# Mixer projections placed between attention units, ada slabs shared out anew, and expert slabs loaded in pairs, in a two-block transformer kernel

## The reference

```python
for l in range(DEPTH):
    mod = (silu(c) @ ada_w[l] + ada_b[l]).reshape(B, 3, 3, D)      # 9 x 1024 columns
    x = x + 0.5 * mod[:, 0, 2] * swiglu(modulate(rms_norm(x), ...), ffn_w_in[l, 0], ffn_w_out[l, 0])
    x = x + mod[:, 1, 2] * token_mix(modulate(rms_norm(x), ...))
    x = x + 0.5 * mod[:, 2, 2] * swiglu(modulate(rms_norm(x), ...), ffn_w_in[l, 1], ffn_w_out[l, 1])
```

```python
y_gdn = gated_deltanet(qkv, z, b_raw, a_raw, ...)   # causal convolution of 4 taps, silu, l2 norms,
                                                    # chunked delta rule over 4 heads of 128, norm, * silu(z)
y_nsa = native_sparse_attention(q, kc, vc, ks, vs, kw, vw, gates, ...)   # 8 heads of 64, rotated
                                                    # three branches: compressed (15 keys), selected, window
return concatenate([y_gdn, y_nsa]) @ w_out
```

## Time and profile before

| | |
|---|---|
| median of 3 runs | 3339.81 us (3338.42 to 3344.32) |
| profiled execution, its own time | 3344.84 us |
| its span | 3343.1 us |
| PE busy | 2922.2 us (87%) |
| DVE busy | 1452.7 us (43%) |
| ACT busy | 787.7 us (24%) |
| slab transfers | 662 of 1024 KB, 2 of 128 KB; 13.4 us from issue to landing |
| read from HBM | 697.84 MB |

### The profile page before, as it was taken

How to read it: one execution, slowest core, us unless ns; L and a number is a source line. 1 busy time by engine, 2 the same in 40 slices (tenths; PEclk the granted TensorE clock), 3 DMA queues, 4 the chain that set the end, 5 groups by cost and what they waited for, 6 DMA issues and landing times.

```text
span 3343.1 us, 43275 instructions
## 1 busy us (share of the span) xinstructions
PE 2922.2 (87%) x17606; PEld 2132.8 (64%) x17606; DVE 1452.7 (43%) x3244; ACT 787.7 (24%) x1477; POOL 0.2 (0%) x4
## 2 busy tenths in 40 slices
PE   6999776699999977679999998998988987999998
PEld 5998675599899867559987565333334675433333
DVE  3867433377676742336521313333333343233333
ACT  3331222243333122224322221101101232110100
POOL 0000000000000000000000000000000000000000
PEclk9999785699999978569999558999999997999999
DMA  8766300156466520014442002999997221799997
GB/s 318 277 232 233 117 1 26 36 210 235 188 254 251 227 101 12 15 41 153 185 148 92 1 9 114 384 420 421 421 421 300 76 102 51 315 421 421 421 421 327
DMA packets 99372, 701.77 MB, mean 210 GB/s; under 512 B 11744, under 2 KB 14176, under 8 KB 14304
## 3 DMA queue, kind: packets, MB, share of 16 engines
q1 hardware_dynamic: 99168, 698.93, 52.5%
HBM read 697.84 MB, written 1.05 MB: 209 GB/s over the span
## 4 chain that ended last, share of the span: by engine, by line
PE 42%; DMA 12%; DVE 4%; ACT 2%; issue 1%; SPq 0%; DVEq 0%; ACTq 0%
DMA ring<-slabs 12%; PE ps L1071 8%; PE ps L684 7%; PE ps L1092 4%; PE ps L1109 3%; PE ps L865 2%; PE ps L678 2%; PE ps L1282 2%; PE ps L1283 2%; PE ps L1284 2%; PE ps L1041 1%; PE ps L852 1%; PE ps L835 1%; PE ps L839 1%; PE ps L1239 1%
## 5 line engine op out<-in xcount | busy, mean ns | idle before, releaser
L1282 PE MATMUL ps<-arena_parts 128*128 128x256 f32 x2112 | 603.1, 286 | 24.1 <-DVE arena_parts L2739 24.1
L1283 PE MATMUL ps<-arena_parts 128*128 128x256 f32 x2112 | 599.1, 284 | 0.0
L1284 PE MATMUL ps<-arena_parts,ring_parts 128*128 128x256 f32 x2112 | 598.2, 283 | 0.0
L1071 PE MATMUL ps<-ring,arena 128*64 128x512 f32 x2048 | 471.6, 603 | 52.7 <-DMA ring<-slabs 47.8
L684 PE MATMUL ps<-h,ring 128*128 128x256 f32 (+1 forms) x1920 | 457.9, 400 | 19.2 <-DVE h L2383 7.6
L684 PEld LDWEIGHTS ps<-h,ring 128*128 128x128 f32 x1920 | 377.2, 198 | 88.1 <-issue 10.9
L1282 PEld LDWEIGHTS ps<-arena_parts 128*128 128x128 f32 x2112 | 403.6, 191 | 25.5 <-issue 25.3
L1284 PEld LDWEIGHTS ps<-arena_parts,ring_parts 128*128 128x128 f32 x2112 | 402.7, 191 | 0.0
L1283 PEld LDWEIGHTS ps<-arena_parts 128*128 128x128 f32 x2112 | 401.9, 190 | 0.2
L1071 PEld LDWEIGHTS ps<-ring,arena 128*64 128x64 f32 x2048 | 148.2, 138 | 302.3 <-issue 296.6
L2655 DVE TENSOR_TENSOR ring_parts<-ring,arena_parts 128x2048 fp32r<-128x2048 f32 x132 | 299.7, 2290 | 91.0 <-ACT arena_parts L1425 91.0
(11 more groups left out here) (347 smaller groups left out, 2773.7 us busy)
## 6 DMA issues: line engine op xcount, KB each, us to landing
ring<-slabs SPq DMA_DIRECT2D x662, 1024.0 KB, 13.4
constants<-const SPq DMA_DIRECT2D x1, 1372.5 KB, 7.6
x<-xT SPq DMA_DIRECT2D x1, 1024.0 KB, 9.8
outT<-x SPq DMA_DIRECT2D x1, 1024.0 KB, 4.7
vectors<-vec SPq DMA_DIRECT2D x1, 747.5 KB, 4.6
ring<-slabs SPq DMA_DIRECT2D x2, 128.0 KB, 5.5
arena<-pos SPq DMA_DIRECT2D x1, 128.0 KB, 7.4
x<-metaT SPq DMA_DIRECT2D x1, 64.0 KB, 9.8
```

What stands on the lines that cost most here:

```text
L1071: mm = nc.tensor.matmul(ps[W * hh:W * hh + W, e % 2, :], xe[:, e % 2, 4 * k + c], wt[:, c], start=(k == 0 and c == 0), stop=(k == 1 and c ...
L1282: nc.tensor.matmul(out, w_hi, v_hi, start=start, stop=False, skip_group_check=True)
L1283: nc.tensor.matmul(out, w_hi, v_lo, start=False, stop=False, skip_group_check=True)
L1284: return nc.tensor.matmul(out, w_lo, v_hi, start=False, stop=stop, skip_group_check=True)
```

## The change

**Mixer.** The order of the slabs becomes `MIX_ORDER`: first the six slabs of the attention (`nq`, `nk`, `vc`, `vtok`, `gba`: 14 jobs), then four of `qkv`, the two of compression, two of `qkv`, two of `z`. After the 14 jobs comes the rotation, then jobs and attention units alternate on PE: jobs 14 and 15; six times one job and one piece; two compression jobs with a piece each; eight times one job and two pieces. A piece is `scores(n + 1)`, `turn(n)`, `values(n - 1)`. Branches go 1, 2, 0. Then `gdn`. DVE puts one convolution ahead of each `softmax_max`, ACT the eviction of the job ahead of `exp`. The attention of the mixer uses banks 4 and 5 for scores, 6 for turns and 7 for values, one set each, because jobs hold 0 to 3. Its output lies in `hid`, its norm and turn are done inside `gdn` after levels 0, 1 and 2. Silu of `z` and of the compression's hidden values no longer happens in the eviction: `z` follows in `gdn` (ACT), the hidden values by an exponential on ACT and three steps on DVE (`hidden_cmp`).

**Ada slabs.** 16 instead of 12 in each of three FFNs, at two a step for the first six steps; 8 in mixer 0, 4 in mixer 1.

**Expert slabs.** Two neighbouring `eup` or `edown` slabs are one transfer of 2 MB, 16 KB a partition, which waits until both slots are free and counts on the even slot's semaphore. There are 192 of them, and 280 single slab loads.

The diff, cut to its core (the forgetting attention keeps its banks and its order):

```diff
+FFN_SHARE = 16
+MIX_ADA = ((1, 1, 2, 2, 1, 1), (1, 1, 1, 1, 0, 0))
+MIX_ORDER = (8, 9, 10, 11, 12, 13, 0, 1, 2, 3, 4, 5, 6, 7)
 def ada_share(l, i, step):
-    for at, layer, first in (((0, 0), 0, ADA_PART), ((0, 1), 1, 0), ((1, 0), 1, ADA_PART)):
+    for at, layer, first in (((0, 0), 0, ADA_PART), ((0, 1), 1, 0), ((1, 0), 1, FFN_SHARE)):
         if (l, i) == at:
-            past = lambda n: first + min(2 * n, n + 2, ADA_PART)
+            past = lambda n: first + min(2 * n, n + FFN_SHARE - 10, FFN_SHARE)
...
         elif st[0] == "mix":
-            for s in range(14):
-                out += [("mixin", st[1], s, "pe")]
-                out += [("ada", st[1], 2 * ADA_PART + s, "dve")] if s < ADA_PART else []
-            out += [("cmpw", st[1], s, "pe") for s in range(2)]
+            for p, i in enumerate(MIX_ORDER):
+                out += [("cmpw", st[1], s, "pe") for s in range(2)] if p == 10 else []
+                out += [("mixin", st[1], i, "pe")] + [("ada", st[1], n, "dve") for n in mix_share(st[1], p)]
...
+def paired(plan, i):
+    return plan[i][0] in ("eup", "edown") and plan[i + 1:i + 2] and plan[i + 1][0] in ("eup", "edown") and i % 2 == 0
...
             def load(i):
                 if i >= RING:
                     name, value = free[i - RING]
                     sp.wait_ge(s[name], value)
+                if paired(plan, i):
+                    name, value = free[i + 1 - RING]
+                    sp.wait_ge(s[name], value)
+                    both = ap["slabs"][i:i + 2].rearrange("n p w -> (n p w)").rearrange("(p w) -> p w", p=P)
+                    sp.dma_start(ring[:, i % RING:i % RING + 2, :].rearrange("p n w -> p (n w)"), both)\
+                        .then_inc(slot_loaded[i % RING], 16)
+                    return
...
# PE, mixer
-                    run_jobs(q, st, 0, 30, slab, job, h_at=("h_ready", n_ready - KC))
...
+                    run_jobs(q, st, 0, 14, slab, job, h_at=("h_ready", n_ready - KC))
+                    n_mix = sum(MIX_ADA[st[1]])
+                    mix_cols(q, st, sum(MIX_ADA[st[1]][:4]), n_mix)
...
                     pe.wait_ge(s["ada_col"], n_share)
+                    pe.wait_ge(s["proj_act"], act_before(q) + 8)
                     nsa_rope(q, st[1])
-                    await_("dve", q, "roped", 3)
+                    scores, piece, n_units = attention(q, st)
+                    for i in range(8):
+                        run_jobs(q, st, 14 + i, 15 + i, slab, job)
+                        if i == 1:
+                            await_("dve", q, "roped", 3)
+                            scores(0)
+                        elif i >= 2:
+                            piece(i - 2)
+                    await_("act", q, "kc2")
+                    for c in range(2):
+                        run_jobs(q, st, 22 + c, 23 + c, slab, job)
+                        piece(6 + c)
+                    nsa_compressed(q, st[1], job)
+                    for i in range(8):
+                        if i == 2:
+                            await_("act", q, "cmp")
+                        run_jobs(q, st, 24 + i, 25 + i, slab, job)
+                        piece(8 + 2 * i)
+                        piece(9 + 2 * i)
+                    piece(n_units)
+                    await_("dve", q, "o", n_units - 1)
                     gdn(q, st[1])
                     await_("dve", q, "y_gdn")
-                    await_("act", q, "kc2")
-                    run_jobs(q, st, 30, 32, slab, job)
-                    nsa_compressed(q, st[1])
-                    await_("act", q, "cmp")
-                    attention(q, st)
-                    turn_outputs(q, st)
                     await_("act", q, "y_att", 1)
                     run_jobs(q, st, 32, 40, slab, job, behind=True)
...
# ACT, mixer
+                    for i in range(8):
+                        evict(24 + i)
+                        for n_unit in (8 + 2 * i, 9 + 2 * i):
+                            exp(n_unit)
+                            copy(n_unit)
+                    gdn(q, st[1])
...
# ACT, gdn
+                act.wait_ge(s["proj_act"], act_before(q) + 26)
+                mark(nc.scalar.activation(view(ZS, 4, T1), view(ZS, 4, T1), ACT.Silu), q, "z")
                 nc.scalar.preload_act_table_set("natural_log_exp_and_others")
...
+                    if lev == 1:
+                        nsa_root(q)
+                    if lev == 2:
+                        take_outputs(q, ("mix", l))
...
# DVE, mixer
+                        softmax_max(0)
+                        for i in range(2, 8):
+                            conv(q, l, i)
+                            softmax_max(i - 1)
+                            if i > 2:
+                                output(i - 3)
...
+                        hidden_cmp(q, 0)
+                        hidden_cmp(q, 1)
+                        for i in range(8):
+                            if i < 4:
+                                conv(q, l, 8 + i)
+                            for n_unit in (8 + 2 * i, 9 + 2 * i):
+                                if n_unit < 23:
+                                    softmax_max(n_unit + 1)
+                                output(n_unit - 1)
+                        output(23)
+                        gdn(q, l, job)
...
# DVE, gdn, after each level
+                    if lev < 2:
+                        nsa_square(q, lev)
+                    if 1 <= lev < 3:
+                        nsa_scale(q, lev - 1)
```

More of the change, by code:

```diff
@@ L349, in host_arrays @@
         v = slab_array(s, a)
-        slabs[i, :, :v.shape[1]] = v
+        if paired(plan, i) or (i and paired(plan, i - 1)):
+            slabs[i - i % 2:i - i % 2 + 2].reshape(P, 2, SLAB)[:, i % 2] = v
+        else:
+            slabs[i, :, :v.shape[1]] = v
     return {
@@ L378, in build @@
     plan = slab_plan(stages)
-    free = releases(plan)
+    free, arrive = releases(plan), arrivals(plan)
     with ExitStack() as ctx:
@@ L467, in _ @@
             for i in range(len(plan)):
-                load(i)
+                if not (i and paired(plan, i - 1)):
+                    load(i)
             name, value = x_written(stages)[-1]
@@ L868, in values, with piece @@
                     mark(mm, q, "pv", n)
-                scores(0)
-                for n in range(len(units) + 1):
+                def piece(n):
                     if n + 1 < len(units):
@@ L877, in attention @@
                         values(n - 1)
+                return scores, piece, len(units)
             def turn_outputs(q, st):
@@ L1387, in _ @@
                     await_("act", q, "ncum")
-                    attention(q, st)
+                    scores, piece, n_units = attention(q, st)
+                    scores(0)
+                    for n_unit in range(n_units + 1):
+                        piece(n_unit)
                     turn_outputs(q, st)
@@ L1898, in _ @@
-                    gdn(q, st[1])
-                    nsa_blocks(q, st[1], job)
-                    hc, cb = view(HC, 2, 2 * NCMP), view(CB, 2)
+                        dst = {"qkv": lambda: qi[:, idx, 3:], "nq": lambda: nqk[:, idx], "z": lambda: zs[:, idx],
+                               "nk": lambda: nqk[:, 4 + idx], "vc": lambda: view(VC, T1)}[kind]()
+                        nc.scalar.copy(dst, bank((job + i) % 4, T1)).then_inc(s["proj_act"], 1)
+                    for i in range(14):
+                        evict(i)
@@ new lines, in _ @@
+                    nc.scalar.preload_act_table_set("natural_log_exp_and_others")
+                    gba_read = job_read[proj_end(q) - 1]
+                    act.wait_ge(s[gba_read[0]], gba_read[1])
+                    mark(nc.scalar.activation(view(SMALL + 128, 2, 28), view(SMALL, 2, 32)[:, :, 0:28], ACT.Exp,
+                                              scale=-1.0), q, "sg")
+                    exp, copy = attention(q, st)
+                    evict(14)
+                    evict(15)
+                    nsa_blocks(q, st[1], job)
@@ L1913, in _ @@
-                    attention(q, st)
-                    nsa_root(q)
-                    take_outputs(q, st)
+                    mark(nc.scalar.copy(view(VCMP, 2 * 64)[0:NCMP], ps[0:NCMP, (job + 23) % 4, 0:2 * 64]), q, "cmp")
+                    for i in range(8):
[4 more added lines that the diff above has]
+                    gdn(q, st[1])
                     for i in split_seq(q + 1, stages[q + 1])[0:2]:
@@ L1920, in _ @@
                     fox_forget(q)
-                    attention(q, st)
+                    exp, copy = attention(q, st)
+                    for n_unit in range(len(attn_units(st))):
+                        exp(n_unit)
+                        copy(n_unit)
                     take_outputs(q, st)
@@ new lines, in _ @@
+                        ada_col(l, 3 * ADA_PART - sum(MIX_ADA[l]), 3 * ADA_PART, ada_slabs)
+                        n_ada += 1
+                        nsa_rope(q, l)
+                        sg = view(SMALL + 128, 2, 28)
```

(5 more changed lines are left out.)

310 lines of the change are left out of this document (170 added, 140 removed).

## The result

The changed kernel takes **3239.1 us** (median of 4 runs, 3236.9 to 3241.0), the kernel before 3342.1 beside it (4 runs): ratio **0.9688**, 95% interval 0.9668 to 0.9709. It is faster, and inside the range of the forecast, but 103 us were saved where 157 were forecast.

The account below looks back on a forecast made before the run. PE bounds the dense stages, DMA holds the last expert stages, and no engine is full in the mixers' attention. Savings 72 + 78 + 5.4 - 4.8 + 6.3 = 157 us give 3183 us against the median; range 3145 to 3250.

Parts of the forecast that it names:

- term 6: Mixer, delta rule: silus, squares and table loads before the first root take 8.5 us; from there to its end 107.3.
- rival A: Clock stays at 1.2 GHz through the mixed stage: 90 us more per mixer, 3363 us in all; chance 4%.
- term 4: Mixer, two compression jobs: 7 us each at full clock, plus units, hidden-value wait and small products; 24.5 us.
- term 5: Mixer, eight iterations of one job and two units: 10.1, 8.7 or 7.0 us each by keys; 65.6 us.
- terms 1 and 2: Mixer 0 start: fourteen jobs before attention 42 us, wait for ada sums 4.5, rotation with two jobs 10.
- The sign that I had set: Mixer: granted clock over 0.85 between job 14 and the last value would show the forecast right.
- Term 3: Mixer, six iterations of one job and one unit: four at 5.65, two at 6.5, 2 for first exponential; 38 us.
- Terms 6 and 7: Mixer, delta rule: 8.5 us to first root, 107.3 to its end, 6 for attention output's norm and turn inside.
- Rival B: Mixers: nothing overlaps, in-order queues leave units their old time and jobs add; 45 us per mixer, 3273 us; chance 10%.
- Output projections: After each mixer, they start with the clock up: about 2.6 us saved each, 5.4 with the norm's first rows.
- Ada slabs: Three FFNs, four more slabs each: 0.4 us of product per slab, 4.8 us added; DVE's work fits the step.
- The pairs: Expert stages: two-slab transfers run 1% faster, 4.6 us per stage, less a later end; 6.3 us saved together.

Follow-up runs that it names:

- Wide: Changed kernel with every matmul of the two compression jobs streaming 114 columns instead of 30 or 1; 3223.4 us, 0.9651 of the kernel before.
- Fillwide: Changed kernel with compression matmuls widened to 114 columns and result-free filling matmuls on PE ahead of turns; 3209.9 us, 0.9608 of the kernel before.
- share12: Changed kernel with the ada slabs put back, 12 in each of three FFNs and 12 in each mixer; 3254.6 us, 0.9741 of the kernel before.
- expfirst: Changed kernel with each unit's exponential ahead of the job's eviction on ACT; 3217.9 us, 0.9638 of the kernel before.
- order: Changed kernel with exponential ahead of eviction on ACT and, in two-unit iterations, the convolution behind both masks on DVE; 3189.3 us, 0.9549 of the kernel before.
- pairs: Kernel before with only the transfers of two expert slabs added; 3329.0 us, 0.9964 of the kernel before.
- the best version: Changed kernel with ACT and DVE reordered, gba products at 128 columns, compression windows at 58, fillers where PE still waits; 3160.2 us, 0.9458 of the kernel before.

## Why the prediction was right or wrong, point by point

By its terms, in us, each with the marks that the forecast itself used (PE's rows; for term 6 the last copy of a turned score on ACT, at 473.4 in mixer 0, and the first root on ACT, at 481.9):

| term | forecast | mixer 0 | mixer 1 |
|---|---|---|---|
| 1, 2: projections, ada wait, rotation, two jobs | 56.5 (50.5) | 61.4 | 55.3 |
| 3: six one-unit iterations | 38 | 34.9 | 34.9 |
| 4: compression jobs | 24.5 | 37.1 | 38.4 |
| 5: two-unit iterations | 65.6 | 77.1 | 77.8 |
| 6: last copy to first root | 8.5 | 8.4 | 8.4 |
| 6, 7: first root to output projections | 113.3 | 112.2 | 112.4 |
| sum | 306.4 (300.4) | 331.2 | 327.1 |

- **The mechanism was right.** Jobs fill the waits of the units, and the clock, 0.50 in `attention` before, is 1.00 in the six iterations. The output projections start at 594, not at 570. No run has the new order of the mixer alone; what it gains is read from the stages.
- **The step that failed is one assumption, and far less the sums:** "PE at its upper level, once jobs are mixed in". I weighed the clock only as rival A, for the whole stage or not at all. It fell in parts. Of the 25 to 27 us missing per mixer, 12.6 to 13.9 are in term 4, where the 64 small rows of a job took 11.5 and 13.7 us, not 7; 11.5 to 12.2 in term 5; 5 in terms 1 and 2, of which 3 in mixer 0 are the rotation at 1.2 GHz (6.1 us, not 3); terms 3, 6 and 7 give 4 back. The sign that I had set, a clock over 0.85 from job 14 to the last value, failed: it was 0.81. Rival A was wrong as a whole (a mean clock of 0.53 in one part, 1.00 in another), but its own formula, 90 x (1/c - 1), gives 21 us a mixer at 0.81, and its price by parts the place: 17 for the compression jobs alone.
- **Term 4 had its warning in the earlier trace rows.** I took 7.01 us for a row group at half clock and halved it, without asking whether rows of 30 and 1 columns would keep the clock that they were to be costed at. Wide shows that they don't, and that as many rows with 114 do.
- **Term 5's 65.6 was too short by 3 us apart from the clock.** From job to job the iterations take 10.5, 10.4, 12.5, 13.1, 9.3 and then three times 7.1 to 7.2 us, where I had 8.7 twice, 10.1 twice and 7.0 four times: the excess is all in the first five, where the clock falls. Fillwide, with the changed kernel's waits and a clock of 0.96 up to the last copy, takes 68.7. So 8.4 of the 11.5 go away with the fillers and the widened columns, and 3.1 are my sum.
- **Term 3 was 3 too long.** The turn does start 1.5 us behind the job. The 2 us for the first exponential don't show, and the fifth iteration (6.0 us, forecast 6.5) runs the values of a unit of 128 keys, since values lag one unit behind the turn; I had costed them as 256.
- **Terms 6 and 7** held within 1.1. I costed a single buffer for scores at nothing. In one-unit iterations that is so. In two-unit ones DVE's mask made waits of 0.2 to 0.7, 1.4 in all, and 5.0 once ACT was out of the way. No run gives the scores a second set of banks.
- **Rival B** (nothing overlaps) was wrong as priced. Its 180 us for parts 2 to 5 stand against 138 by the forecast's own terms, not 135, so the price was 42 per mixer. Measured are 162 in mixer 0, a little over half way. Its mechanism, foreign instructions ahead of each link on the in-order queues, is what expfirst and order remove: 24 us of 331 in mixer 0.
- **Output projections:** 2.6 of the 5.4. `gdn` ends with waits (5.0 us for DVE just ahead), so the clock is down again when they start.
- **Ada slabs:** 10 by the stage table, 7.8 by share12, instead of 4.8. I had DVE at 17.3 of 18.05 us per step and said "it fits"; it is late in the sixth step in a row, for 1 us in FFN (0,1) and (1,0), which with the slower rows behind it makes 2.7 and 1.1. Of the rest 0.9 stands ahead of the first ada product in FFN (0,1), with 16 slabs as with 12.
- **The pairs:** 13.3 instead of 6.3, of which 11.4 are theirs alone (run pairs). The value was above my upper bound of 1.4% from the earlier trace rows, not the 1% that I took: 14.93 to 14.69 us an expert is 2.49 to 2.45 us a slab, 1.6%. The tail was there (a wait of 1.24 us for the last pair). The page "DMA: Bandwidth & Descriptors" of the Trainium skill, by whose fabric ceiling my estimate was 25, would have given twice what came.

## What to carry to other kernels

Cost a small matmul at the clock that it leaves behind, not at the one that it finds: in this kernel rows with few columns and short waits both went with a low clock, and the dense work next to them paid. Where a matmul's time is its weight load (as here, where rows of 32, 114 side by side and 128 columns all take 0.117 us at full clock), widen its moving operand with columns nobody reads, if they lie close together; and in a loop where PE alternates with ACT and DVE, put the link PE waits for ahead of the eviction that can wait. A wait taken away in such a loop gave back nearly twice its length where the clock was low, and its length where it was up, so look at the granted clock by part, not by stage, before and after.

## What the runs showed of the hardware that I had not expected

- The clock falls and rises several times in one mixer, with no wait of PE over 2.1 us between the rotation and the last value (the longest is 2.02). It stood at 0.53 through rows of 30 and 1 columns with PE 90% busy (33.34 of 37.10 us), and at 1.00 in rows of 58 and 114 columns in their place. Behind rows of 32 columns the rotation of mixer 1 took 4.90 us, behind rows of 128 columns 3.29.
- A moving operand read at a stride of 16 bytes costs: 114 columns take 0.21 us a row at full clock (6.72 for 32), against 0.117 side by side, and 58 at a stride of 32 bytes are at 0.118. The Trainium skill's page "SBUF — State Buffer", under its "Door 1: The DMA port swizzle", says that each access to a new 16-byte line pays a penalty; this case's traces agree in the first case. In the second no penalty shows: at the 1.84 ns a column of the first (0.21 us over 114, an estimate), 58 columns would take 0.107 us, less than the 0.118 that a row takes anyway.
- A transfer of 2 MB in 16 KB rows ran at 427 to 428 GB/s against 421 to 422 for two of 1 MB, both with a full queue.

What stays open: why the clock comes back sooner in one place than in another (the first job of the two-unit part took 5.1 us in the changed kernel and 6.5 in expfirst), and the delta rule, where it is still 0.83 in the best version and whose waits (25.4 us in six for DVE, in order) were not filled.
